# Segment sums of a chunked scan: two groups ahead of the gate product, the others two groups late, with ScalarE making their arguments

## The reference, cut to what matters

```python
def ssd_chunked(xs, log_a, bm, cm, init_state):
    ...
    a = jnp.moveaxis(log_a.reshape(b, nc, SSD_CHUNK, G, E), 2, -1)
    a_cs = jnp.cumsum(a, axis=-1)
    lmat = jnp.exp(segsum(a))
    cb = jnp.einsum("bclgn,bcsgn->bcgls", cm, bm)
    y_diag = jnp.einsum("bcgls,bcgels,bcsgep->bclgep", cb, lmat, xs)
    decay_states = jnp.exp(a_cs[..., -1:] - a_cs)
    states = jnp.einsum("bclgn,bcgel,bclgep->bcgepn", bm, decay_states, xs)
    ...
    y_off = jnp.einsum("bclgn,bcgepn,bcgel->bclgep", cm, prev_states, jnp.exp(a_cs))
    return (y_diag + y_off).reshape(b, L, G, E, P), final_state
```

## Time and profile before

| what | value |
|---|---|
| median of 3 runs | 3430.28 us (3428.87 to 3430.92) |
| the profiled execution's own time | 3430.17 us, its span 3428.3 us |
| PE, DVE, ACT, POOL busy over the span | 95%, 70%, 48%, 15% |
| the eight x turns of the scan | from about 1811 us to 2013.8 us of the span |

### The profile page before, as it was taken

How to read it: one execution, slowest core, us unless ns; L and a number is a source line. 1 busy time by engine, 2 the same in 40 slices (tenths; PEclk the granted TensorE clock), 3 DMA queues, 4 the chain that set the end, 5 groups by cost and what they waited for, 6 DMA issues and landing times.

```text
span 3428.3 us, 43309 instructions
## 1 busy us (share of the span) xinstructions
PE 3271.1 (95%) x13510; PEld 2317.7 (68%) x13510; DVE 2395.1 (70%) x2867; ACT 1659.0 (48%) x2238; POOL 514.5 (15%) x626
## 2 busy tenths in 40 slices
PE   8989999999989999989999999799999999999997
PEld 3453677774453777755645657688888888888885
DVE  4874655453964746455548984688988988998886
ACT  3332433222341423233221133488888888888884
POOL 0000000000000000000000000233443443444340
PEclk9989999999989999999999999899999999999999
DMA  5101334321101333321110022599999999999995
GB/s 200 61 31 43 110 118 141 117 92 54 52 30 49 129 135 117 117 89 55 47 54 26 25 79 87 183 360 360 369 374 362 367 375 362 364 376 365 361 373 201
DMA packets 168014, 618.37 MB, mean 180 GB/s; under 512 B 18528, under 2 KB 18656, under 8 KB 167328
## 3 DMA queue, kind: packets, MB, share of 16 engines
q1 hardware_dynamic: 157232, 573.90, 46.1%
q0 software_dynamic: 10672, 43.00, 4.4%
HBM read 587.99 MB, written 28.84 MB: 180 GB/s over the span
## 4 chain that ended last, share of the span: by engine, by line
PE 88%; DVE 9%; ACT 2%; issue 1%; POOL 0%; DMA 0%; DVEq 0%; POOLq 0%; ACTq 0%; SPq 0%
PE bank L602 52%; PE bank L1238 31%; PE bank L1228 1%; DVE sb_work L1925 1%; DVE sb_rstd L1887 1%; PE bank L1246 1%; PE bank L1189 1%; DVE sb_work L2073 0%; DVE sb_work L2431 0%; DVE sb_work L2387 0%; PE bank L1181 0%; PE bank L964 0%; DVE sb_work L2093 0%; DVE sb_work L2325 0%; PE bank L793 0%
## 5 line engine op out<-in xcount | busy, mean ns | idle before, releaser
L2665 DVE TENSOR_TENSOR w_part<-sb_ring,w_part 128x1024 fp32r<-128x1024 f32 x762 | 900.1, 1231 | 96.3 <-ACT w_part L1787 91.5
L1787 ACT ACTIVATE w_part<-sb_ring 128x1024 fp32r<-128x1024 f32 x762 | 779.0, 1055 | 136.5 <-PE bank L1238 77.3
L1238 PE MATMUL bank<-w_part,xg_hi 128*128 128x512 f32 x2048 | 563.9, 397 | 0.0
L602 PE MATMUL bank<-h_hi,split_part 128*128 128x512 f32 x1408 | 444.4, 400 | 7.9 <-ACT h_hi L1518 7.9
L1238 PEld LDWEIGHTS bank<-w_part,xg_hi 128*128 128x128 f32 x2048 | 382.9, 188 | 89.3
L1238 PE MATMUL bank<-w_part,xg_lo 128*128 128x512 f32 x1024 | 321.0, 395 | 0.0
L602 PEld LDWEIGHTS bank<-h_hi,split_part 128*128 128x128 f32 x1408 | 265.7, 190 | 80.5 <-issue 15.6
L1238 PE MATMUL bank<-w_part,act_hi 128*128 128x512 f32 x1024 | 284.7, 399 | 0.1
L602 PE MATMUL bank<-sb_hT,sb_ring 128*128 128x512 f32 x576 | 261.4, 611 | 11.7 <-ACT sb_hT L1339 11.7
L602 PE MATMUL bank<-h_lo,split_part 128*128 128x512 f32 x704 | 272.3, 394 | 0.0
L602 PE MATMUL bank<-act_hi_ff,split_part 128*128 128x512 f32 x704 | 229.1, 407 | 5.7 <-DVE act_lo_ff L2246 5.7
(11 more groups left out here) (363 smaller groups left out, 4633.4 us busy)
## 6 DMA issues: line engine op xcount, KB each, us to landing
sb_ring<-in_w SPq DMA_DIRECT2D x768, 512.0 KB, 8.3
sb_ring<-in_wstream SPq DMA_DIRECT2D x304, 512.0 KB, 3.6
y_rows<-sb_padc POOLq DMA_DIRECT2D x1, 4096.0 KB, 17.7
sb_xT<-in_x SPq DMA_DIRECT2D x4, 512.0 KB, 7.3
x_rows<-sb_padc SPq DMA_DIRECT2D x1, 2048.0 KB, 9.6
residual<-sb_hT POOLq DMA_DIRECT2D x1, 2048.0 KB, 6.5
sb_hT<-residual POOLq DMA_DIRECT2D x1, 2048.0 KB, 7.9
x_rows<-sb_work SPq DMA_DIRECT2D x1, 2048.0 KB, 6.6
```

Of the source, the lines that this page charges most:

```text
L602: ins = nc.tensor.matmul(out, l, r, start=start, stop=stop)
L1238: ins = nc.tensor.matmul(out[n][:], l[:, k, :], r[:, n * 512:(n + 1) * 512], start=False, stop=(k, p) == (KD - 1, 2))
L1787: nc.scalar.activation(w_hi[t % SPLITS], ring[:, t % RING, :], ACT.Copy).then_inc(s_hi, 1)
L2665: nc.vector.tensor_tensor(w_lo[t % SPLITS], ring[:, t % RING, :], w_hi[t % SPLITS].bitcast(F32), ALU.subtract).then_inc(s_lo, 1)
```

## The change

It moves `segments(0)` and `segments(1)` ahead of the gate product (and, in turn 4, ahead of the pool product), and lets the segment sums of groups 2 and 3 follow `within(0)` and `within(1)`. The arguments `seg_in` are made by ScalarE instead of VectorE: for each group six copies of the 128x128 mask, each scaled by the decay column of one head (`seg_args`). ScalarE makes those of group g + 2 after the exponentials of group g; after groups 2 and 3 it makes those of groups 0 and 1 of the next turn. The z of the gate is taken out of its bank after the exponentials of group 1 instead of ahead of those of group 0.

```diff
@@ TensorE @@
                            *(("cb", s) if g == GROUPS - 1 else ()))
-                    if s in POOL_BEFORE:
-                        pool_projection(POOL_BEFORE[s])
-                    gate_projection(*divmod(s - 2 * CB, TB))
-
                     def segments(g):
-                        pe.wait_ge(dve_done, when("seg_in", s, g))
+                        pe.wait_ge(act_done, when("seg_in", s, g))
...
                     segments(0)
+                    segments(1)
+                    if s in POOL_BEFORE:
+                        pool_projection(POOL_BEFORE[s])
+                    gate_projection(*divmod(s - 2 * CB, TB))
                     for g in range(GROUPS):
...
                     pe.wait_ge(dve_done, when("xs", s))
                     for g in range(GROUPS):
-                        if g + 1 < GROUPS:
-                            segments(g + 1)
                         within(g)
+                        if g + 2 < GROUPS:
+                            segments(g + 2)
@@ ScalarE @@
+            def seg_args(s, g):
+
+                d, _, b = SCAN[s]
+                a = d * SSD_HEADS + g * HPG
+                for e in range(HPG):
+                    nc.scalar.activation(seg_in[:, g % 2, e * P:(e + 1) * P], const(("upto", "from")[d]), ACT.Copy,
+                        scale=la[:, b, a + e:a + e + 1]).then_inc(act_done, did.up(("seg_in", s, g)))
+
+            act.wait_ge(dve_done, when("la"))
+            for g in range(2):
+                seg_args(2 * CB, g)
             for s, (d, kind, b) in enumerate(SCAN):
-                if s in POOL_BEFORE:
+                if kind == "c" and s in POOL_BEFORE:
                     pool_out(POOL_BEFORE[s])
                 if kind == "x":
                     i = s - 2 * CB
-                    act.wait_ge(s_res, 16)
-                    act.wait_ge(pe_done, when("full", "z", *divmod(i, TB)))
-                    act.wait_ge(act_done, did.n)
-                    nc.scalar.activation(hT[:, i, :], bank_of("z", *divmod(i, TB))[:], ACT.Copy).then_inc(act_done,
-                        did.up(("free", "z") + divmod(i, TB)))
                     for g in range(GROUPS):
+                        if g == 2:
+                            if s in POOL_BEFORE:
+                                pool_out(POOL_BEFORE[s])
+                            act.wait_ge(s_res, 16)
+                            act.wait_ge(pe_done, when("full", "z", *divmod(i, TB)))
+                            act.wait_ge(act_done, did.n)
+                            nc.scalar.activation(hT[:, i, :], bank_of("z", *divmod(i, TB))[:], ACT.Copy).then_inc(
+                                act_done, did.up(("free", "z") + divmod(i, TB)))
                         if g >= 2:
                             act.wait_ge(pe_done, when("full", "yd", s, g - 2))
...
+                        if g < 2:
+                            seg_args(s, g + 2)
+                        elif s + 1 < len(SCAN):
+                            seg_args(s + 1, g - 2)
@@ VectorE @@
-                    def seg_arg(g):
-                        if g >= 2:
-                            dve.wait_ge(pe_done, when("full", "seg", s, g - 2, 1))
-                        a = d * SSD_HEADS + g * HPG
-                        dve.wait_ge(dve_done, did.n)
-                        nc.vector.tensor_tensor(seg_in[:, g % 2, :].rearrange("p (h t) -> p h t", t=P), la[:, blk,
-                            a:a + HPG].unsqueeze(2).to_broadcast([P, HPG, P]), mask.unsqueeze(1).to_broadcast([P,
-                            HPG, P]), ALU.mult).then_inc(dve_done, did.up(("seg_in", s, g)))
-
...
-                    seg_arg(0)
-                    seg_arg(1)
...
                     decayed(0)
-                    seg_arg(2)
                     scaled_carry(0)
                     scaled_carry(1)
                     decayed(1)
-                    seg_arg(3)
                     scaled_carry(2)
```

## The result

The changed kernel takes 3436.61 us (median of 13 runs, 3435.47 to 3441.24) against 3430.28 us (13 runs), a ratio of 1.0021 with a 95% interval of 1.0014 to 1.0029. It is slower, by 6.3 us where 9.0 were forecast.

What follows compares the result with a forecast made beforehand. The prediction took TensorE's chain with waits at the turn's end as the bound, not VectorE's fullness. A 1.36 us bank wait and 0.41 us copies, less 0.22 and 0.27 returned, gave 1.28 us a turn: 3439.1 us, range 3434 to 3444.5.

Steps and rivals of the forecast that it cites:

- What bounds the kernel: Steady turn of 24.89 us: TensorE needs 23.44 us without waits; 1.45 us are waits in the turn's last 6 us.
- VectorE's busy share: Rival: VectorE's fullness bounds the turn; with 4.3 us less, 23.44 us a turn, 3420 us in all; chance 0.07.
- The bank: Fourth segment product, behind st: its bank waits for the first state add, a new 1.36 us in seven turns.
- The copies: ScalarE, between exponentials of groups 2 and 3: six copies take 1.95 us and make group 3's exponentials 0.41 us late.
- The turn: One steady scan turn, start of st to the next: 26.17 us against 24.89, 1.28 us more.
- the sum: Whole kernel: seven turns add 7 x 1.28 = 8.96 us to 3430.17, giving 3439.1 us.
- Nothing is late in turn 4: Turn 4: no bank wait, since the first bank is free at 1810.6 and wanted at 1813.8.
- The shift reaches the end: Behind the scan: TensorE bounds the rest and nothing waits for a fixed time, so all 8.96 us stay.

Runs made afterwards that it cites:

- the first experiment: The changed kernel with segments(1) moved back behind the gate product, segments(0) still ahead of it; 3436.33 us, ratio 1.0018.
- copies alone: The kernel before with arguments made by ScalarE, the next turn's behind group 3's exponentials, and TensorE's order unchanged; 3430.41 us, ratio 1.0000.
- copies behind: The changed kernel with ScalarE's copies for the next turn's group 0 behind the exponentials of group 3; 3437.84 us, ratio 1.0021.
- both costs undone: The changed kernel with segments(1) behind the gate and the next turn's copies behind the exponentials of group 3; 3431.38 us, ratio 0.9999.
- the change, twice: The changed kernel and its repeat without edit; 3436.61 us, ratio 1.0021, then 3438.60 us, ratio 1.0024.
- decay early: Third experiment: the changed kernel with VectorE's state decay moved from ahead of the state adds to behind the fourth scaled_carry; 3431.27 us, ratio 1.0004.
- before, longer wait: The kernel before with VectorE's add_within(1) moved from behind xw to ahead of decayed(3); 3437.59 us, ratio 1.0019.
- xw early: The changed kernel with VectorE's xw moved from behind decayed(3) to behind the fourth scaled_carry; 3424.43 us, ratio 0.9983.
- xw early, copies behind: The changed kernel with xw behind the fourth scaled_carry and the next turn's copies behind group 3's exponentials; 3420.24 us, ratio 0.9970.
- st ahead of within(3): The kernel of "both costs undone" with xw and state decay behind the fourth scaled_carry and st ahead of within(3); 3428.88 us, ratio 0.9994.
- no waits: "xw early, copies behind" plus st ahead of within(3), segments(1) behind the gate, decay ahead of decayed(3), add_within(3) behind state adds; 3417.21 us, ratio 0.9962.

## Why the prediction was right

**What bounds the kernel: right.** The turn is a chain through the end of the turn and a ring of banks, and VectorE's busy share was no bound: with 4.3 us less on it and the old order the turn fell by 0.50 us, to 24.39, not by 1.45.

**The bank: right, and right in size.** Forecast 6.87 us behind `st` for the fourth segment product, measured 6.79; and for the gate behind it 7.53, measured 7.54. Taking it away on TensorE's side or on VectorE's side gave the same turn, 24.70 us, 1.39 less than the change.

**The copies: right in kind, the delay a third too dear.** Forecast 1.95 us for six and 0.41 us of delay; measured 1.85 and 0.31. The estimates from the figures of the Trainium skill (ScalarE: Activation LUTs, section on what a table load costs) were 0.39 us a copy, 1.85 for six and 0.31 of delay; the trace agrees, with 0.389 us a copy.

**The turn:** forecast 26.17, measured 26.08 to 26.09 where the clock held. Seven times 1.2 is 8.4 us; the sum said 9.0. The difference is the copies' 0.10 us a turn: it shows ahead of `within(3)`, which starts 0.75 us later than its work allows (forecast 0.9), while `st` starts 0.50 us late as forecast. The profile shows 0.59 and 0.24 us of idle time there, since the modelled ends reach into these waits.

**"Nothing is late in turn 4": right** on the bank; in the first profiled execution a fall at the `st` ahead of it cost 1.6 us, which the prediction had no term for.

**"The shift reaches the end": not fully.** The medians are 6.3 us (13 runs) and 7.9 us (10 runs) above before. Inside the scan the last `xw` is 9.5 us late in the second profiled execution; 2.4 of that are back at the end, at two later waits behind which the clock came back sooner. The prediction had taken the rest of the program as unable to give anything back.

**What was missing altogether is the clock.** It was read as 1.00 in the scan before and taken for granted. Three or four falls came with the change; those followed by a bank wait hid it and so cost only 0.2 to 0.3 us. That the sum came out so near is in part luck: the bank wait happened to hide the falls, and what the clock gave back behind the scan was of the same small size. In the first experiment, where nothing hid them, four of them took back 4 x 1.68 = 6.7 us of the 9.0 that the turns gave (six times 1.39, and 0.64 from turn 4 to turn 5, where `within(0)` of turn 4 also waits 0.55 us).

## What to carry to other kernels

An output that is moved forward in TensorE's order also moves forward in the ring of banks: ask which bank it takes over and when that one's last reader is done, not only whether its inputs are ready. An engine that is 90% busy need not be the bound; move its work out of the chain that ends the turn (here `xw`, 1.76 us, which went into its idle time). Whether that alone would have helped the kernel before, without the hand-over, was not run. And compare the turn, not only the time: two medians can be equal because a saving was lost elsewhere.

## What the runs showed of the hardware that was not expected

TensorE's clock fell in a stage in which TensorE was busy for 24.14 of 26.09 us, with no wait longer than about 1.1 us. The count over the eight x turns of each profiled execution, with the waits that TensorE's rows show at the end of the turn:

```
kernel                          ahead of within(3)   ahead of st   falls
before                          0.17 us              0.24 us       0
copies alone; copies behind     0.29 us              0.24 us       1; 1
both costs undone               0.29 us              0.24 us       3
the change, twice               0.59 us              0.24 us       3; 3
decay early; segments(1) late   0.59 us              0.24 us       3; 4
before, longer wait             0.83 us              0.24 us       5
xw early                        0.59 us              none          0
xw early, copies behind         0.29 us              none          0
st ahead of within(3)           1.15 (within(2))     none          0
no waits                        none                 none          0
```

Each of these falls lies at an `st` that had itself waited, 1.8 us behind another wait; in the four kernels in which `st` follows without a wait there is none, even with one wait of 1.15 us. The falls at the `st` of turn 3, which waits 2.55 us for its `xw` in every kernel, are not counted; four profiles have one. A fall costs 1.6 to 1.7 us if nothing hides it. Which `st` it strikes, and how many, differs between executions of one kernel (the change, twice). That the pair of short waits brings the fall is shown as far as lengthening the first of them in the kernel before brings five, and removing the second removes all, along with other changes to the turn; what the chip counts isn't shown, and one profile a kernel is few. Nor do the waits say which turns fall, since they are the same in every turn: in the first and third experiments the slow `st` stand 51.0 to 51.1 us apart, in the two profiles of the change 78.2 to 78.6. So the place of a turn in time seems to play a part too, and a kernel without a fall in its one profile may have had its turns placed well; that rival is open for the four kernels without a wait ahead of `st`. The Trainium skill (TensorE: Matmul & The Clock Gate, section on a second failure mode with PSUM-queue cycling) says of another kernel, with bf16 products of 512 columns, that frequent short idles between groups of products were enough to make the clock swing between its two levels. These rows agree in so far as falls in these turns came only where two short waits stand close together; the pair of 0.17 and 0.24 us brought none, and neither did a single wait.
